# Masked attention levels spread over the last rows of a unit instead of standing in one run behind it

## What is computed

```python
h = rmsnorm(x, norm_mix)
q, k, v, r, g_lr, hy_in = split(h @ w_in)
x = x + concat([gla_group(q, k, v, r, g_lr, ...), hyena_group(hy_in, ...)]) @ w_out
h = rmsnorm(x, norm_ffn)
x = x + (silu(h @ w_gate) * (h @ w_up)) @ w_down
```

```python
S_t = diag(exp(g_t)) S_{t-1} + k_t^T v_t ;  o_t = q_t S_t
```

## Time and profile before

| | |
|---|---|
| time of 3 runs | 1371.45, 1371.91, 1377.22 us (median 1371.91) |
| the profiled execution | 1371.01 us, its span 1369.2 us |
| PE busy | 1333.2 us (97%) in 9152 matmul records |
| ACT, DVE, POOL busy | 492.9, 414.8, 649.6 us |
| granted clock of PE | 0.994 of full speed over the span |
| masked levels (L1296) | 2560 matmul records, 25.6 us busy |

### The profile page before, as it was taken

The page is one execution under the profiler, slowest core; times in us unless marked ns, Lnnn a source line. Parts: engine busy times, 40 slices in busy tenths (PEclk is TensorE's granted clock), DMA queues, the critical chain, the costliest instruction groups (busy, mean ns, idle before and its releaser), DMA issues.

```text
span 1369.2 us, 21223 instructions
## 1 busy us (share of the span) xinstructions
PE 1333.2 (97%) x9152; PEld 1069.9 (78%) x9152; DVE 414.8 (30%) x681; ACT 492.9 (36%) x804; POOL 649.6 (47%) x395
## 2 busy tenths in 40 slices
PE   6899999999999999999999999999999999999997
PEld 5666777788888778888886777778888888888886
DVE  5842756425022110000054665474320000000003
ACT  4644433444322222221246543434442322232122
POOL 2644542273555455554423854415535555555442
PEclk9999999999999999999999999999999999999999
DMA  5211111122322222322311211111312232332231
GB/s 222 78 63 48 45 51 63 47 92 96 107 92 93 88 82 94 122 93 92 105 65 47 79 63 48 63 47 62 108 62 93 96 104 93 99 117 92 97 104 77
DMA packets 31196, 115.98 MB, mean 85 GB/s; under 512 B 3456, under 2 KB 3712, under 8 KB 30720
## 3 DMA queue, kind: packets, MB, share of 16 engines
q1 hardware_dynamic: 31104, 114.63, 24.9%
HBM read 112.52 MB, written 2.10 MB: 84 GB/s over the span
## 4 chain that ended last, share of the span: by engine, by line
PE 91%; DVE 4%; ACT 2%; issue 1%; POOL 1%; DMA 1%; POOLq 0%; SPq 0%; DVEq 0%; ACTq 0%
PE ps L1147 18%; PE ps L1148 17%; PE ps L1149 17%; PE ps L1169 5%; PE ps L1166 5%; PE ps L1167 5%; PE ps L1361 4%; PE ps L1376 2%; PE ps L1234 2%; PE ps L1188 2%; PE ps L1163 2%; PE ps L1296 2%; PE ps L1160 2%; PE ps L1158 2%; PE ps L1221 1%
## 5 line engine op out<-in xcount | busy, mean ns | idle before, releaser
L727 POOL TENSOR_TENSOR w_lo<-w_raw,w_hi 128x1024 fp32r<-128x1024 f32 x192 | 459.7, 2395 | 534.8 <-ACT w_hi L432 534.8
L1147 PE MATMUL ps<-h_hi,w_hi 128*128 128x512 f32 (+1 forms) x1064 | 430.4, 404 | 1.1 <-DVE g L935 0.6
L1149 PE MATMUL ps<-h_hi,w_lo 128*128 128x512 f32 (+1 forms) x1064 | 413.3, 388 | 0.0
L1148 PE MATMUL ps<-h_lo,w_hi 128*128 128x512 f32 (+1 forms) x1064 | 413.2, 388 | 0.0
L432 ACT ACTIVATE w_hi<-w_raw 128x1024 fp32r<-128x1024 f32 x192 | 201.8, 1051 | 198.8 <-PE ps L1169 194.5
L1147 PEld LDWEIGHTS ps<-h_hi,w_hi 128*128 128x128 f32 x1064 | 200.4, 188 | 50.3 <-issue 9.2
L1148 PEld LDWEIGHTS ps<-h_lo,w_hi 128*128 128x128 f32 x1064 | 200.4, 188 | 45.5 <-issue 6.9
L1149 PEld LDWEIGHTS ps<-h_hi,w_lo 128*128 128x128 f32 x1064 | 200.2, 188 | 41.9
L1121 DVE TENSOR_TENSOR hid<-ps,sg 128x512 f32<-128x512 f32 x44 | 30.4, 692 | 428.7 <-PE ps L1149 428.7
L790 POOL TENSOR_TENSOR hid_lo<-hid,hid_hi 128x512 fp32r<-128x512 f32 x44 | 57.3, 1301 | 126.0 <-ACT hid_hi L705 126.0
L705 ACT ACTIVATE hid_hi<-hid 128x512 fp32r<-128x512 f32 x44 | 27.8, 632 | 203.3 <-DVE hid L1121 203.3
(11 more groups left out here) (181 smaller groups left out, 1575.5 us busy)
## 6 DMA issues: line engine op xcount, KB each, us to landing
w_raw<-in_units SPq DMA_DIRECT2D x198, 512.0 KB, 3.4
gain<-in_gain SPq DMA_DIRECT2D x5, 512.0 KB, 4.6
par<-in_par SPq DMA_DIRECT2D x2, 1118.5 KB, 8.4
x<-in_x SPq DMA_DIRECT2D x4, 512.0 KB, 7.2
out_y<-x SPq DMA_DIRECT2D x4, 512.0 KB, 2.6
cst<-in_cst SPq DMA_DIRECT2D x1, 1280.0 KB, 13.4
cst<-in_cst SPq DMA_DIRECT2D x1, 224.0 KB, 3.8
mask_f<-in_mask SPq DMA_DIRECT2D x1, 160.0 KB, 11.0
```

Source lines behind the costliest of these rows:

```text
L727: nc.gpsimd.tensor_tensor(w_tile(g, 1), w_raw[:, g % RAW], w_tile(g, 0).bitcast(F32), ALU.subtract).then_inc(s_lo, 1)
L1147: nc.tensor.matmul(out, hi, act_hi, start=start, stop=False)
L1148: nc.tensor.matmul(out, hi, act_lo, start=False, stop=False)
L1149: return nc.tensor.matmul(out, lo, act_hi, start=False, stop=stop)
```

## The change

The masked levels get a function of their own, one level a call, and a unit's row loop calls it: levels 3 and 4 of step 2 behind the sixth and the seventh row, level 6 of step 3 behind the seventh row. The last level of a step (5 or 7) stays behind the last row, ahead of or among the unit's side work as before. Each level waits for its own `xld`; the wait for `big` or `put` goes with the first level of a step, so it now stands behind the sixth or the seventh row. The matmuls, their operands and their number stay the same. `s_unit` is raised by the last row as before, which now stands behind two or one of the levels.

```diff
+            def masked_level(L, h, l):
+                p = STEP_OF[l]
+                pe.wait_ge(xld.sem, xld.at(L, lvl(h, l) + 1))
+                if l == STEPS[p][0]:
+                    if p == 2:
+                        pe.wait_ge(big.sem, big.at(L, h + 1))
+                    else:
+                        pe.wait_ge(put.sem, put.at(L, 10 * h + PUTS[p]))
+                xl = ring[:, lvl(h, l) % FACT]
+                for n in range(TT):
+                    for e in range(0, P, NEAR):
+                        cols = slice(P * n + e, P * n + e + NEAR)
+                        at = level_cols(l).start + NEAR * n
+                        for way in range(2):
+                            rows = slice(DK * way, DK * way + DK)
+                            last = nc.tensor.matmul(ps[e:e + NEAR, LA + way, at:at + NEAR], xl[rows, cols], xl[rows, cols],
+                                                    start=True, stop=True)
+                if l == STEPS[p][-1]:
+                    last.then_inc(pair.sem, 1)
+
             def level_step(L, h, p):
+                if p >= 2:
+                    masked_level(L, h, STEPS[p][-1])
+                    return
...
-                else:
-                    if p == 2:
-                        pe.wait_ge(big.sem, big.at(L, h + 1))
-                    else:
-                        pe.wait_ge(put.sem, put.at(L, 10 * h + PUTS[p]))
-                    for l in STEPS[p]:
-                        xl = ring[:, lvl(h, l) % FACT]
...
                         if k == 3:
                             side(L, t, 0)
+                        step = step_at(t - 4)
+                        if step and step[1] >= 2 and k in (5, 6):
+
+                            levels = STEPS[step[1]][:-1]
+                            if k - 7 + len(levels) >= 0:
+                                masked_level(L, step[0], levels[k - 7 + len(levels)])
                     last.then_inc(s_unit, 1)
                     side(L, t, 1)
```

## The result

The changed kernel takes 1376.76 us (median of 8 runs, 1374.12 to 1378.79) against 1372.54 of the kernel before beside it: ratio 1.0027, 95% interval 1.0017 to 1.0038, so 3.7 us (2.3 to 5.2) slower. Measured once more among the experiments the same kernel gave 1.0012 (1.0000 to 1.0025). Both are within the 0.5% that I called no change; the first is clear of zero, the second touches it, and the forecast of +2.6 lies between them. Executions of one kernel differ by some us with the mean clock that PE was granted: those of before at 0.992 of full speed took 1373.5 to 1376.1 us, those at 0.997 1369.5 to 1370.4.

What follows compares the result with a forecast made beforehand. PE was taken to bound the kernel, busy 97% of the span. Breaks +8.2, cover -0.7, wait +0.4 and stops -5.2 made +2.7 on 1371.0, so 1373.7; against the median 1374.5 us was forecast, range 1369 to 1379.5.

Steps and rivals of the forecast that it cites:

- Breaks: Masked steps on PE: 24 more switches between row and small matmuls, 0.34 us each, 8.2 us (bounds 4.8 and 10.8).
- The two covered breaks: After head 3 in each layer PE waits for DVE anyway, so moving level 6 there is free: -0.7 us.
- The wait for `big`: Ahead of row 7, layer 1 head 0: ACT's last copy ends late, one stop of 0.4 to 0.5 us.
- Rival 2: The waits grow: five units with little room stop PE, 4.3 us more, 1378.8 us; chance 0.08.
- the later `s_unit`: Signal comes 2.0 or 1.0 us later, followers up to 1.3 us later against PE; costed at nothing.
- Stops: Three-level runs: PE's program arrives late in 256-instruction blocks, 6.2 us; 5.2 us go, 1.0 stays.
- a sign against it: In the after trace's changed units, no "issue" stop over 1 us was to appear if the forecast was right.
- the need: From PE reaching the earlier block boundary to going on, in the four stopping runs: 3.1, 2.3, 3.8 and 1.4 us.
- Rival 1: Stops in three-level runs stay, fewer than 1.0 of 6.2 us go: +7.9 us, 1379.8 us; chance 0.14.
- rival 3: Breaks at masked levels cost only 0.20 us and the stops all go: -1.4 us, 1370.5 us; chance 0.14.

Runs made afterwards that it cites:

- e1_shift: The kernel before with 16 small matmuls (64 instructions with their loads) added in the first slot of layer 0; one time, 1375.5 us.
- the second profile: The changed kernel itself measured and profiled once more, among the experiments: 1374.88 us, ratio 1.0012 to the kernel before.
- e4_steps_of_3: Half of the change to the kernel before: only levels 3 and 4 moved, levels 6 and 7 in one run; 1372.73 us, ratio 0.9998.
- e5_steps_of_2: The other half of the change to the kernel before: only level 6 moved, behind the seventh row; 1373.73 us, ratio 1.0005.
- e7_pad_final: The kernel before with 48, 8, 84 and 64 instructions of repeated matmuls (layer 0 head 1; layer 1 heads 0, 2, 3): 1366.45 us, ratio 0.9952.
- e6_pad_best: The kernel before with 48, 84 and 64 instructions of repeated matmuls (layer 0 head 1; layer 1 heads 2, 3): 1366.07 us, ratio 0.9951.

## Why the prediction was right

*The account.* Forecast +2.7 us against the profiled execution, +2.6 against the median; the spans differ by 4.9 behind the start, the two measurements say 3.7 and 1.6. The order of the terms was right, and the sum was 2.2 us short: 1.7 of that is the stops, 0.4 the breaks, 0.1 the wait.

*Breaks.* 0.34 taken, 0.36 measured at every lone level; 8.6 us for 8.2. The two covered breaks gave back 0.33 and 0.37, as said.

*The wait for `big`.* Layer 1, head 0 alone, 0.47 for the 0.4 to 0.5 expected; the units with next to no room (0.15 us in layer 1, head 2) had no wait. Rival 2 did not come: no other matmul of a masked level has DVE or ACT as releaser, so the later `s_unit` cost nothing that PE shows.

*Stops.* The cause was right: shown by the shift, by blocks used up to the instruction, and by 5 us won with more work (some 1.6 of it by the clock). The size was not: 2.7 us (2.3 in the second profile) stayed instead of 1.0. One stop of over 1 us was left, which the prediction had named as a sign against it. The step that failed is "of the need about 2.8 remains (1.0 of the 3.8 is spent on the row ahead of it)". That takes a row ahead of the boundary to help as much as one behind it. In after the boundary there is passed at 842.27, with level 4's first matmul, and the packet starts at 843.65, 1.4 us behind it and not before:

```profile
DMA  0030090000000000000000000000000000000000
...
q8 instruction: 1, 0.02, 4.8%
```

(DMA of after, 843.5 to 844.7, slices of 0.03 us; the sixth slice is the packet's start.) It takes 0.92 us (4.8% of 16 engines over 1.2 us), and the next instruction starts at 846.09, 3.8 us behind the boundary: what that unit needed in before. (So too in the second profile: boundary at 840.96, going on at 844.78.) A row ahead of the boundary bought nothing, the one behind it its full 1.0 us: 2.76 became 1.70. With the need kept at 3.8, 3.8 - 2.1 = 1.7 comes out of my own sum. The 0.48 of layer 0, head 1, expected at nothing, is another error: the need was taken as fixed, 3.1 us, and it was 3.6 in after, 3.3 in its second profile, 4.3 in e4_steps_of_3 and 3.3 in e5_steps_of_2, where nothing in the unit had moved. What sets it stays open. And I missed layer 1, head 1, where the block that ends in level 4 now holds one row fewer (0.32, and nothing in the second profile).

*What the sum left out.* The 1.6 us at half clock behind the longest stop. Had that stop shrunk to 0.8 as forecast, they might have gone with it, and the forecast gave no term for that; as both kernels paid them, the sum came out unharmed, by luck.

*Rival 1* (the stops stay: 3.5 of 6.2 us went) is out, *rival 3* (a break of 0.20) too. The part of the range above the forecast was the one that was needed.

The Trainium skill, "Runtime: NRT & Kernel Launch", section "Instruction fetch mechanics", is right here on blocks of 256 instructions. Its statement that fetching is hidden does not hold where 256 instructions last 1.1 us: up to 2.8 us of PE were lost at one boundary.

## What to carry to other kernels

A break between large and small matmuls has a price (here 0.36 us), and cutting a run in three to spread it pays only if the run had a cost of its own that the pieces lose. Idle time on PE that no semaphore explains, inside a run of very short instructions, is worth a look at the instruction queue and at the count of instructions between two such gaps. If the count is a multiple of 256, move the boundary with a few harmless instructions before rebuilding the schedule: that was 5 to 7 us here by the times (3.9 to 4.4 between the marks in the profiles), with work added, where the rebuilt schedule lost 2 to 4. And look at the granted clock behind a long gap: the gap may cost more than it lasts.

## What the runs showed of the hardware

PE's program comes in 16 KB packets of 256 instructions. At the 24 stops of these ten profiles that the timeline shows with their idle time, PE went on 1.2 to 1.5 us after the end of the packet that had started last, which took 0.9 to 1.4 us (in after: start 843.65, end 844.57, going on at 846.09). The packet started between 1.0 us before and 1.6 us after PE passed the earlier boundary, so from that boundary to going on it was 1.4 us (before, near 214) to 4.3 us (e4_steps_of_3, near 134). That the late block is what holds PE is read from these distances and from the spacing by 256; no row shows the hold itself. In the feed-forward stage, where a block lasts about 28 us, PE never stopped for it.

A stop can cost more than it lasts. Behind 2.56 us of idle time in before, 1.50 in after, 2.05 and 2.32 in e5_steps_of_2 PE was granted 1.2 instead of 2.4 GHz for some 3.4 us. It didn't follow every such gap: not the 1.78 us in before, nor the 2.55 us in e1_shift (842.99).

The start of the kernel is not steady. The same instructions bring PE to the first masked run's place 2.2 us earlier (e7_pad_final) or 2.2 us later (e6_pad_best) than in before. One part is the load of the gains: the first PE matmul starts between 9.3 and 10.3 us. The other is the clock: ahead of that place before has two stretches of some 3.4 us at half clock, e7_pad_final one, e6_pad_best three. Two profiles are better compared from a common instruction on than by their spans.
